# Three spill buffers, earlier first loads and rescheduled row operations in the last stage of a two-block transformer kernel

## Chip, cores and metric

The kernel runs on one core of a Trainium2 chip. The metric is the device time of one execution in microseconds (us); lower is better. The number compared is the median over several runs.

## What is computed

The reference applies two transformer blocks to a sequence of 512 tokens of width 1024, in float32. The first block has two kinds of attention and a mixture of experts; the second has a state space branch, an attention with forgetting and, last, a "PEER" layer. Only that last layer is touched by the change:

```python
def peer_ffn(h, w_query, sub_keys, u_tab, v_tab):     # 8 heads, 128 x 128 = 16384 experts, top 16
    q = (h @ w_query).reshape(bsz, seq, PEER_HEADS, 2, PEER_HALF)
    scores = jnp.einsum('blhcd,hckd->blhck', q, sub_keys)
    s_top, i_top = lax.top_k(scores, PEER_TOPK)
    # sums of all pairs of the two halves, then the best 16 pairs a head -> expert_idx, gates
    ...
        u_sel = u_tab[i_blk]
        act = jax.nn.gelu(jnp.einsum('td,thkd->thk', h_blk, u_sel))
        w = g_blk * act
        return jnp.einsum('thk,thkd->td', w, v_tab[i_blk])
```

## The kernel before

**Two ways through the same layer.** The 512 tokens are four tiles of 128. For three tiles (384 tokens, `DENSE`) the kernel computes all 16384 dot products with the table u, multiplies them by gates that are zero where an expert was not chosen, and multiplies the result w by the whole table v. The fourth tile (tile 0, `SPARSE`) is done by gathers: 128 selected rows of u and 128 of v for each token, one row per token at a time. Such a "row operation" (`row_work`) is one gather of 128 rows of 1024 float32, half a megabyte, issued by GpSimd (`gather`), and one multiply-accumulate on VectorE over 128x1024. There are 256 of them, 128 with u (L2486) and 128 with v (L2490).

**The loops.** Step n runs from 0 to 127. Steps 0 to 63 are the u loop, steps 64 to 127 the v loop (`NG` = 64). Each step needs one megabyte of a table: SyncE (its queue is called SP) loads it into one of two slots of `uv_raw` (`load`, two steps ahead), ScalarE copies it rounded into `uv_hi` (`high`, L2299), VectorE makes the remainder `uv_lo` (`low`, L2495), and TensorE multiplies in three passes (L123 to L125). A slot of `uv_raw` is free when `low` has read it; a slot of `uv_hi` when TensorE has finished the step two before.

**The u loop.** Each step gives two groups m of 128x384 activations. `gelu` (L2336, ScalarE) writes each into `a_out[:, m % NA, :]` and SP stores it to the DRAM tensor `a_rows`. Before `gelu(m)` may write, the store of m - NA must have landed, and TensorE must not start group m before `gelu(m - 2)`. In steps 0 to 45 VectorE selects experts (units "T" of `plan`), and in steps 22 to 58 VectorE, ScalarE and GpSimd make one-hot tables ("H", L2148 on GpSimd, L2471 and L2473 on VectorE) that TensorE multiplies into gates (L2245). ScalarE collects these in `spread` (L2310) and stores it twelve times, two megabytes each, to `g_rows`; the first write after such a store waits until it has landed.

**The v loop.** Step n = 64 + p needs w of pair p. SP loads the activations back (`a_rows` into a half of the old `qT4`, 384 KB for each p) and every fourth p also the gates of eight keys (`g_rows`, 1.5 MB), both by `load_weights(p)`. VectorE multiplies them (`wf`, L2505), ScalarE rounds (`w_hi`, L2303), VectorE subtracts (`w_lo`, L2510). `load_weights(p)` waits for `wf` of p - 2, whose slot it overwrites.

**The orders.** Each engine runs its instructions in program order, and so does each issuing queue. In its loop over n, SP issues `load(n + 2)`, then the two stores of step n, and then, from n = `NG - 2` on, `load_weights(n - (NG - 2))`. VectorE begins a step with `low(n + 1)`, then does the T and H work of that step, then the row operations that `plan` gives; in the v loop `weights` and one row operation stand between. GpSimd makes the one-hots of a step and then issues its gathers; a gather into a home waits for the VectorE operation that used this home before.

**The tables of numbers.** `rows_in` says how many row operations stand in each step. `MIDDLE_AT` and `LATE_AT` say from which row operation on the four homes in `keysT` and `work`, and the one in `rows_c`, may be used beside the five early ones: the first four are busy until the selection ends with step 45, the last until all gates are stored.

```python
    rows_in = {n: 1 for n in range(12, 22)} | {22: 3, 34: 4} | {n: 4 for n in range(46, NG)}
    rows_in |= {NG + k: 2 if k % 3 == 2 else 3 for k in range(NG - 1)}
```

Of the kernel before, what the change touches and what calls it, by code (L numbers as in the profile page):

```python
# [18 lines left out]
P = 128  # L19
# [16 lines left out]
PH, PK, PT16 = 8, 128, 16  # L36
# [39 lines left out]
def build_program(nc, t, out):  # L76
    with ExitStack() as ctx:
        emit(nc, t, out, ctx)


def emit(nc, t, out, ctx):
    era = []

    def sem(name):
        stack = ctx.enter_context(ExitStack())
        s = stack.enter_context(nc.semaphore(name))
        era.append((stack, s))
        return s

    def clear_semaphores():  # L90

        with nc.Block() as block:
            @block.gpsimd
            def _(pool):
                for _, s in era:
                    pool.sem_clear(s)
        for stack, _ in era:
            stack.close()
        era.clear()

    def sb(stack, name, shape, dt=F32):
        return stack.enter_context(nc.sbuf_tensor(name, shape, dt))
# [24 lines left out]
    class Gemm:  # L127
# [12 lines left out]
        def each(self, eng, body):  # L140

            base = 0
            for g, (count, width, _) in enumerate(self.segments):
                behind = self.segments[g + 1][1] if g + 1 < len(self.segments) else None
                if count > 1:
                    with eng.Fori(0, count - 1) as i:
                        body(i + base, g, i, width, width)
                body(base + count - 1, g, count - 1, width, behind)
                base += count
# [299 lines left out]
    stage = ExitStack()  # L449
# [387 lines left out]
    stage = ExitStack()  # L837
# [9 lines left out]
    stage = ExitStack()  # L847
# [332 lines left out]
    stage = ExitStack()  # L1180
    HW = KT // 2 * CH
    RAW, SPLIT, AHEAD, UNITS = 6, 3, 3, 12
# [286 lines left out]
    stage = ExitStack()  # L1469
# [63 lines left out]
    stage = ExitStack()  # L1533
# [22 lines left out]
    for at, kind in enumerate(CHUNKS):  # L1556
# [4 lines left out]
        for k in range(0, depth, per):  # L1561
            units.append((at, kind, src[:, k * width:(k + per) * width], range(k, k + per), width, k == 0, k + per == depth))
    NU = len(units)
    last_of = {at: x for x, (at, *_, last) in enumerate(units) if last}
    U_END, F_END, G0, Z0, Q0 = last_of[0], last_of[1], last_of[1] + 1, last_of[5] + 1, last_of[9] + 1
    s_ss, s_sq, s_root, s_g, s_h, s_tp, s_tpe, s_tph = (
# [377 lines left out]
    stage = ExitStack()  # L1944
# [42 lines left out]
    NG = P // GROUP  # L1987
# [9 lines left out]
    def uv_source(n):  # L1997
        return t["peer_u_2"][n, :, :] if n < NG else t["peer_v_2"][:, n - NG, :]
# [10 lines left out]
    stage = ExitStack()  # L2009
# [9 lines left out]

    stage = ExitStack()  # L2020
    uv_hi, uv_lo = (sb(stage, f"uv_{x}", [P, 2, GROUP * D], F32R) for x in ("hi", "lo"))
    NA = 2
    a_out = sb(stage, "a_out", [P, NA, DENSE])
    work = sb(stage, "work", [P, 8 * PT16 * PT16])
    rest = work[:, 0:8 * P].rearrange("p (n k) -> p n k", n=4)
# [1 line left out]
    match = work[:, :].rearrange("p (h k j) -> p h k j", h=PH, k=PT16)  # L2027
    top_s = sb(stage, "top_s", [P, 2 * PH, PT16])
    top_k = sb(stage, "top_k", [P, 2 * PH, PT16], U32)
    top_kf = sb(stage, "top_kf", [P, 2 * PH, PT16])  # L2030
    best_s = sb(stage, "best_s", [P, PH, PT16])
    best_p = sb(stage, "best_p", [P, PH, PT16], U32)
    part_p = sb(stage, "part_p", [P, PH, PT16], U32)
# [15 lines left out]
    with ExitStack() as routing:  # L2049
# [12 lines left out]
                                   "gates_spread", "gates_stored"))  # L2062
    s_ast = [sem(f"peer_act_stored{s}") for s in range(NA)]
    s_gin, s_ain = ([sem(f"peer_{x}{s}") for s in range(2)] for x in ("gates_here", "act_here"))
# [5 lines left out]
    EARLY = [x_sb[:, m, :] for m in range(1, TT)] + [rows_a[:, b, :] for b in range(2)]  # L2070
    MIDDLE = [keys_flat[:, b * D:(b + 1) * D] for b in range(2)] + [work[:, b * D:(b + 1) * D] for b in range(2)]
    LATE = [rows_c[:, 0, :]]
    MIDDLE_AT, LATE_AT = 20, 98
    homes = EARLY + MIDDLE + LATE
    s_row = [sem(f"row_here{b}") for b in range(len(homes))]
    home_of, use_of, before_of, last, uses = [], [], [], [-1] * len(homes), [0] * len(homes)
# [8 lines left out]
    turns_at = {x: [at + k for k in range(11)] for x, at in enumerate((0, 11, 23, 35))}  # L2085
    hots_in = [[2, 3, 3] * 4, [2, 3, 3] * 4, [2, 3] * 6 + [2]]
    hots_from = (22, 34, 46)
    rows_in = {n: 1 for n in range(12, 22)} | {22: 3, 34: 4} | {n: 4 for n in range(46, NG)}
    rows_in |= {NG + k: 2 if k % 3 == 2 else 3 for k in range(NG - 1)}
    plan, count, at = [[] for _ in range(2 * NG)], [0] * TT, 0  # L2090
    for x in range(TT):
        for n in turns_at[x]:
# [30 lines left out]
    for g in range(2 * SEL):  # L2123
        n = work_step[before_of[g]] if before_of[g] >= 0 else max(turns_at[SPARSE]) + 1
        if g >= MIDDLE_AT:
            n = max(n, max(turns_at[TT - 1]) + 1)
# [8 lines left out]
    with nc.Block() as block:  # L2135
# [38 lines left out]
        @block.sync  # L2174
        def _(sp):
            def load(n):
                if n >= 2:
                    sp.wait_ge(s_lo, n - 1)
                sp.dma_start(uv_raw[:, n % 2, :], uv_source(n)).then_inc(s_uv[n % 2], 16)

            def load_weights(p):
                if p == 0:
                    sp.wait_ge(s_scr, 4 * TT)
                    sp.wait_ge(s_gst, 16 * HALVES)
                if p >= 2:
                    sp.wait_ge(s_wf, p - 1)
                if p % (GKEYS // GROUP) == 0:
                    q = p // (GKEYS // GROUP)
                    sp.dma_start(g_in[:, q % 2, :].rearrange("p (h x) -> p h x", h=HALVES),
                                 g_rows.rearrange("h p x -> p h x")[:, :, q * GKEYS * HALF:(q + 1) * GKEYS * HALF])\  # L2190
                      .then_inc(s_gin[q % 2], 16)
                for m in (2 * p, 2 * p + 1):
                    sp.wait_ge(s_ast[m % NA], 16 * (m // NA + 1))
                sp.dma_start(a_in[:, p % 2, :, :], a_rows.rearrange("m p n -> p m n")[:, 2 * p:2 * p + 2, :])\
                  .then_inc(s_ain[p % 2], 16)

            for n in range(2 * NG):
                if n + 2 < 2 * NG:
                    load(n + 2)
                if n < NG:  # L2200
                    for m in (2 * n, 2 * n + 1):
                        sp.wait_ge(s_gelu, m + 1)
                        sp.dma_start(a_rows[m, :, :], a_out[:, m % NA, :]).then_inc(s_ast[m % NA], 16)
                if NG - 2 <= n < 2 * NG - 2:
                    load_weights(n - (NG - 2))
                if n == 2 * NG - 8:
                    sp.dma_start(x_back[:, :, :], x_rest).then_inc(s_xb, 16)
            outs = out.rearrange("a (m p) d -> p (a m) d", p=P)
            sp.wait_ge(s_rd, 2 * SEL)
            sp.dma_start(outs[:, 0, :], x_sb[:, 0, :]).then_inc(s_outd, 16)  # L2210
            for m in range(1, TT):
                sp.wait_ge(s_add, 2 * m)
                sp.dma_start(outs[:, m, :], x_back[:, m - 1, :]).then_inc(s_outd, 16)
            sp.wait_ge(s_outd, 16 * TT)
# [77 lines left out]
        def _(act):  # L2292
# [39 lines left out]
            def gelu(m):  # L2332
                act.wait_ge(s_pa, m + 1)
                if m >= NA:
                    act.wait_ge(s_ast[m % NA], 16 * (m // NA))
                act.activation(a_out[:, m % NA, :], ps[:, m % 2, 0:DENSE], ACT.Gelu_apprx_tanh).then_inc(s_gelu, 1)  # L2336
# [277 lines left out]
```

## Time and profile before

| | |
|---|---|
| median of 3 runs | 3783.2 us (3781.36 to 3788.04) |
| the profiled execution | 3781.3 us, of it the span of the trace 3779.5 us |
| u loop, first to last `uv_lo` | 2515 us to 3175 us from the span's start |
| v loop | 3183 us to the end |
| TensorE busy | 3353.4 us, 89% of the span |
| bytes moved by DMA | 954.87 MB, mean 253 GB/s |

The time is that of the whole kernel; the change touches its last third. A duration in the trace belongs to one profiled execution. TensorE's matmuls overlap, so a busy TensorE is not one at its peak; what counts is how far apart the steps are.

### The profile page before, as it was taken

To read this page: it belongs to the slowest core of one execution; us is meant where nothing else is said; L and a number is where in the kernel's file an instruction comes from. 1 tells how busy PE (TensorE), PEld (TensorE's weight loads), DVE (VectorE), ACT (ScalarE), POOL (GpSimd) and SP (SyncE) were. 2 spreads that over 40 slices of the span, in tenths; PEclk is the share of its full clock that TensorE was granted. 3 is DMA by queue.
4 is the path that set the end of the run, shared out by engine and by line. 5 is a ranking of instruction groups with operands and counts; after the bars stand their busy time and mean duration, and the time that the engine had idled before them with its cause. 6 is when DMAs were issued, how large, how long until landed. Compare 5 with 4: busy or idle time off the path is not lost. (4 is left out here: it accounts for less than half of the span.)

```text
span 3779.5 us, 46793 instructions
## 1 busy us (share of the span) xinstructions
PE 3353.4 (89%) x16253; PEld 2811.9 (74%) x16253; DVE 2726.5 (72%) x3557; ACT 1872.1 (50%) x2136; POOL 739.1 (20%) x524
## 2 busy tenths in 40 slices
PE   7697754999999999999299977799999996999998
PEld 3485543888888888887198856589999986777777
DVE  8316545999999999999444226348987776788887
ACT  1225413777777777777124334233478763333332
POOL 0000002011011011010200000001333585455552
PEclk9898867999999999999599978899999998999999
DMA  7520106999999999998633301235655699999996
GB/s 295 179 71 2 46 30 245 386 385 384 385 384 381 388 383 383 388 386 343 232 101 93 95 17 45 73 132 203 219 190 187 247 367 368 339 381 366 369 378 262
DMA packets 217466, 954.87 MB, mean 253 GB/s; under 512 B 23344, under 2 KB 85040, under 8 KB 142448
## 3 DMA queue, kind: packets, MB, share of 16 engines
q1 hardware_dynamic: 161872, 734.91, 51.9%
q0 software_dynamic: 46816, 167.80, 11.9%
q10 hardware_dynamic: 8640, 50.34, 3.3%
q8 instruction: 84, 1.38, 0.1%
q14 instruction: 54, 0.44, 0.0%
HBM read 864.92 MB, written 88.05 MB: 252 GB/s over the span
## 5 line engine op out<-in xcount | busy, mean ns | idle before, releaser
L1395 DVE TENSOR_TENSOR w_low<-w_raw,w_high 128x2048 fp32r<-128x2048 f32 x399 | 907.3, 2288 | 72.8 <-ACT w_high L1324 70.8
L1324 ACT ACTIVATE w_high<-w_raw 128x2048 fp32r<-128x2048 f32 x399 | 765.7, 1919 | 302.4 <-PE ps L125 162.4
L123 PE MATMUL ps<-w_high,xT_high 128*128 128x512 f32 x1056 | 428.8, 406 | 21.3 <-issue 21.3
L2495 DVE TENSOR_TENSOR uv_lo<-uv_raw,uv_hi 128x2048 fp32r<-128x2048 f32 x128 | 294.1, 2298 | 177.1 <-ACT uv_hi L2299 176.6
L124 PE MATMUL ps<-w_low,xT_high 128*128 128x512 f32 x1056 | 412.4, 391 | 0.0
L125 PE MATMUL ps<-w_high,xT_low 128*128 128x512 f32 x1056 | 412.3, 390 | 0.0
L123 PE MATMUL ps<-h4T_high,uv_hi 128*128 128x384 f32 x1024 | 353.5, 345 | 15.1 <-ACT a_out L2336 9.2
L123 PE MATMUL ps<-uv_hi,w_hi 128*128 128x512 f32 x768 | 305.2, 397 | 45.8 <-DVE w_lo L2510 24.9
L125 PE MATMUL ps<-h4T_high,uv_lo 128*128 128x384 f32 x1024 | 344.1, 336 | 0.0
L124 PE MATMUL ps<-h4T_low,uv_hi 128*128 128x384 f32 x1024 | 343.9, 336 | 0.0
L2299 ACT ACTIVATE uv_hi<-uv_raw 128x2048 fp32r<-128x2048 f32 x128 | 244.6, 1912 | 149.7 <-PE ps L125 120.5
L124 PE MATMUL ps<-uv_lo,w_hi 128*128 128x512 f32 x768 | 303.7, 395 | 0.0
L125 PE MATMUL ps<-uv_hi,w_lo 128*128 128x512 f32 x768 | 303.5, 395 | 0.0
L123 PEld LDWEIGHTS ps<-w_high,xT_high 128*128 128x128 f32 x1056 | 199.8, 189 | 60.1 <-issue 22.0
L1213 POOL COPY cur<-slot_ids 128x1 int32 (+1 forms) x34 | 41.1, 1210 | 1029.6 <-PE ps L1265 1026.2
L125 PEld LDWEIGHTS ps<-w_high,xT_low 128*128 128x128 f32 x1056 | 198.8, 188 | 42.6
L124 PEld LDWEIGHTS ps<-w_low,xT_high 128*128 128x128 f32 x1056 | 199.3, 189 | 39.6
L123 PE MATMUL ps<-w_high,hidT_high 128*128 128x512 f32 x528 | 218.1, 413 | 0.0
L123 PEld LDWEIGHTS ps<-h4T_high,uv_hi 128*128 128x128 f32 x1024 | 193.6, 189 | 18.8 <-DVE uv_lo L2495 7.9
L123 PEld LDWEIGHTS ps<-uv_hi,w_hi 128*128 128x128 f32 x768 | 147.1, 192 | 81.0 <-issue 50.5
L125 PE MATMUL ps<-w_high,hidT_low 128*128 128x512 f32 x528 | 206.3, 391 | 0.0
L124 PE MATMUL ps<-w_low,hidT_high 128*128 128x512 f32 x528 | 206.1, 390 | 0.0
(516 smaller groups left out, 7048.9 us busy)
## 6 DMA issues: line engine op xcount, KB each, us to landing
w_raw<-in_w_gate_up SPq DMA_DIRECT2D x267, 1024.0 KB, 6.8
w_raw<-in_w_down SPq DMA_DIRECT2D x132, 1024.0 KB, 7.2
uv_raw<-in_peer_u SPq DMA_DIRECT2D x64, 1024.0 KB, 5.4
uv_raw<-in_peer_v SPq DMA_DIRECT2D x64, 1024.0 KB, 9.5
wbuf_ada<-in_w_ada SPq DMA_DIRECT2D x12, 2048.0 KB, 8.7
a_rows<-a_out SPq DMA_DIRECT2D x128, 192.0 KB, 2.4
g_rows<-spread ACTq DMA_DIRECT2D x12, 2048.0 KB, 8.7
qT<-g_rows SPq DMA_DIRECT2D x16, 1536.0 KB, 15.1
```

The source lines that it names most:

```text
L123: pe.matmul(out, l_hi, r_hi, start=first, stop=False)
L124: pe.matmul(out, l_hi, r_lo, start=False, stop=False)
L125: return pe.matmul(out, l_lo, r_hi, start=False, stop=last)
L1213: pool.tensor_copy(cur[:, :], slot_ids[:, ds(j, 1)]).then_inc(s_cur, 1)
L1324: act.activation(w_hi[:, n % SPLIT, :], w_raw[:, n % RAW, :], ACT.Copy).then_inc(s_wh, 1)
L1395: dve.tensor_tensor(w_lo[:, n % SPLIT, :], w_raw[:, n % RAW, :], w_hi[:, n % SPLIT, :].bitcast(F32), ALU.subtract).then_inc(s_wl, 1)
L2299: act.activation(uv_hi[:, n % 2, :], uv_raw[:, n % 2, :], ACT.Copy).then_inc(s_hi, 1)
L2495: dve.tensor_tensor(uv_lo[:, n % 2, :], uv_raw[:, n % 2, :], uv_hi[:, n % 2, :].bitcast(F32), ALU.subtract).then_inc(s_lo, 1)
```

## The change

Seven numbers or places change. `a_out` has three slots instead of two, and the copy `top_kf` of the selected keys is written over `top_s` instead of having memory of its own. `rows_in` has one row operation in each of the steps 12 to 45 (four in steps 22 and 34), then three and four in turn up to step 63, then two and three in turn. Counted out, steps 12 to 45 hold 40 row operations instead of 17, steps 46 to 63 hold 63 instead of 72, and the v loop holds 153 instead of 167. `MIDDLE_AT` and `LATE_AT` follow. `load_weights(p)` stands one step earlier in SP's program, and ahead of that step's stores instead of behind them.

```diff
-    NA = 2
+    NA = 3
...
-    top_kf = sb(stage, "top_kf", [P, 2 * PH, PT16])
+    top_kf = top_s
...
-    MIDDLE_AT, LATE_AT = 20, 98
+    MIDDLE_AT, LATE_AT = 44, 112
...
-    rows_in = {n: 1 for n in range(12, 22)} | {22: 3, 34: 4} | {n: 4 for n in range(46, NG)}
-    rows_in |= {NG + k: 2 if k % 3 == 2 else 3 for k in range(NG - 1)}
+    rows_in = {n: 1 for n in range(12, 46)} | {22: 4, 34: 4} | {n: 3 + n % 2 for n in range(46, NG)}
+    rows_in |= {NG + k: 3 if k % 2 else 2 for k in range(NG - 1)}
...
+            AHEAD = 3
             for n in range(2 * NG):
                 if n + 2 < 2 * NG:
                     load(n + 2)
+                if NG - AHEAD <= n < 2 * NG - AHEAD:
+                    load_weights(n - (NG - AHEAD))
                 if n < NG:
                     for m in (2 * n, 2 * n + 1):
                         sp.wait_ge(s_gelu, m + 1)
                         sp.dma_start(a_rows[m, :, :], a_out[:, m % NA, :]).then_inc(s_ast[m % NA], 16)
-                if NG - 2 <= n < 2 * NG - 2:
-                    load_weights(n - (NG - 2))
```

SP's queue where the u loop ends, before the change, from the loading of u's last slice (the first row) on. `in_peer_v` is the table v; the gates and activations of p = 0 are the rows that write `qT`:

```order
L2179 DMA uv_raw<-in_peer_u 128x2048
L2203 DMA a_rows<-a_out 128x384 x2
L2179 DMA uv_raw<-in_peer_v 128x2048
L2203 DMA a_rows<-a_out 128x384 x2
L2189 DMA qT<-g_rows 128x12x256
L2194 DMA qT<-a_rows 128x2x384
L2179 DMA uv_raw<-in_peer_v 128x2048
L2203 DMA a_rows<-a_out 128x384 x2
L2194 DMA qT<-a_rows 128x2x384
L2179 DMA uv_raw<-in_peer_v 128x2048
```

The same place after the change:

```order
L2179 DMA uv_raw<-in_peer_u 128x2048
L2189 DMA qT<-g_rows 128x12x256
L2194 DMA qT<-a_rows 128x2x384
L2206 DMA a_rows<-a_out 128x384 x2
L2179 DMA uv_raw<-in_peer_v 128x2048
L2194 DMA qT<-a_rows 128x2x384
L2206 DMA a_rows<-a_out 128x384 x2
L2179 DMA uv_raw<-in_peer_v 128x2048
L2194 DMA qT<-a_rows 128x2x384
L2206 DMA a_rows<-a_out 128x384 x2
```

The gates and the activations of p = 0 have moved ahead of two pairs of stores and of the first slice of v; throughout the v loop `load_weights(p)` now stands ahead of `load(p + 64)` instead of behind it.

VectorE in the middle of the u loop, from the last one-hots of step 27 over the whole of step 28, before the change:

```order
L2471 TENSOR_SCALAR first_hot<-iota_row,selT 128x128
L2473 TENSOR_TENSOR second_hot<-iota_row,selT 128x512
L2495 TENSOR_TENSOR uv_lo<-uv_raw,uv_hi 128x2048
L2397 MAX best_s<-work 128x8 x4
L2400 MAX_INDEX best_p<-best_s,work 128x8 x4
L2417 TENSOR_TENSOR work<-top_s 128x256 x4
L2386 MAX best_s<-work 128x8 x4
L2471 TENSOR_SCALAR first_hot<-iota_row,selT 128x128
L2473 TENSOR_TENSOR second_hot<-iota_row,selT 128x512
```

The same stretch after the change:

```order
L2472 TENSOR_SCALAR first_hot<-iota_row,selT 128x128
L2474 TENSOR_TENSOR second_hot<-iota_row,selT 128x512
L2487 SCALAR_TENSOR_TENSOR rows_a,row_dot<-rows_a,h_s 128x1024
L2496 TENSOR_TENSOR uv_lo<-uv_raw,uv_hi 128x2048
L2398 MAX best_s<-work 128x8 x4
L2401 MAX_INDEX best_p<-best_s,work 128x8 x4
L2418 TENSOR_TENSOR work<-top_s 128x256 x4
L2387 MAX best_s<-work 128x8 x4
L2472 TENSOR_SCALAR first_hot<-iota_row,selT 128x128
L2474 TENSOR_TENSOR second_hot<-iota_row,selT 128x512
```

One row operation (L2487) now stands between the last one-hots of a step and the next `uv_lo`; the work of the selection is the same.

GpSimd's queue after step 22, before the change; the 64 one-hots are those of steps 23 to 45:

```order
L2163 DMA x_sb<-in_peer_u_rows,row_id 128x1024 x3
L2148 TENSOR_SCALAR first_hot<-iota_row,selT 128x128 x32
L2163 DMA rows_a<-in_peer_u_rows,row_id 128x1024 x2
L2148 TENSOR_SCALAR first_hot<-iota_row,selT 128x128 x32
L2163 DMA keysT<-in_peer_u_rows,row_id 128x1024 x2
L2163 DMA work<-in_peer_u_rows,row_id 128x1024 x2
```

The same place after the change, the first few of those steps:

```order
L2163 DMA rows_a<-in_peer_u_rows,row_id 128x1024 x2
L2148 TENSOR_SCALAR first_hot<-iota_row,selT 128x128 x2
L2163 DMA x_sb<-in_peer_u_rows,row_id 128x1024 x3
L2163 DMA rows_a<-in_peer_u_rows,row_id 128x1024
L2148 TENSOR_SCALAR first_hot<-iota_row,selT 128x128 x3
L2163 DMA rows_a<-in_peer_u_rows,row_id 128x1024
L2148 TENSOR_SCALAR first_hot<-iota_row,selT 128x128 x3
L2163 DMA x_sb<-in_peer_u_rows,row_id 128x1024
L2148 TENSOR_SCALAR first_hot<-iota_row,selT 128x128 x2
```

Between the one-hots of two steps GpSimd now issues a gather, which waits for the row operation that used its home before.

## Rows read from the trace of the kernel before

**Rows 1.** Windows: bounds and length, busy us, clock, DMA share, GB/s.

```profile
2717.00:2984.00 267.00, 258.08 (x1669) 254.40 (x1668) 223.15 (x591) 212.50 (x387) 96.55 (x68) 1.00 0.52 190
2984.00:3188.00 204.00, 185.51 (x1138) 182.09 (x1136) 150.93 (x223) 128.23 (x222) 162.76 (x107) 0.98 0.93 356
3188.00:3210.00 22.00, 1.17 (x4) 0.83 (x3) 4.12 (x6) 2.78 (x3) 5.51 (x5) 0.57 1.04 399
...
3240.00:3745.00 505.00, 480.00 (x2066) 393.41 (x2065) 419.21 (x364) 158.70 (x117) 246.81 (x149) 0.98 0.99 371
```

**Rows 2.** Timeline of ScalarE in the v loop: start, us; idle before, releaser.

```profile
3261.26 1.92 ACT L2299 ACTIVATE uv_hi<-uv_raw 128x2048 fp32r<-128x2048 f32 x1 [2.17 <-PE ps L125]
...
3269.42 1.92 ACT L2299 ACTIVATE uv_hi<-uv_raw 128x2048 fp32r<-128x2048 f32 x1 [2.17 <-PE ps L125]
...
3281.07 1.91 ACT L2299 ACTIVATE uv_hi<-uv_raw 128x2048 fp32r<-128x2048 f32 x1 [1.50 <-DMA uv_raw<-in_peer_v]
```

**Rows 3.** All `uv_lo` from 3230.5 to 3750 us: first and last start.

```profile
L2495 DVE TENSOR_TENSOR uv_lo<-uv_raw,uv_hi x60: 2281/2293/2296, 3230.6 to 3749.0; 128x2048 fp32r<-128x2048 f32 x60
```

**Rows 4.** Waits in the v loop, 3240 to 3745 us: total, times, longest.

```profile
DVE wf L2505 <- DMA qT<-a_rows: 26.3, 10, 4.7
PE ps L123 <- DVE w_lo L2510: 24.9, 10, 4.6
```

**Rows 5.** Timeline of SP in the v loop around one load of gates.

```profile
3257.37 0.34 SPq L2179 DMA_DIRECT2D uv_raw<-in_peer_v  x1
3258.23 0.36 SPq L2189 DMA_DIRECT2D qT<-g_rows  x1
3258.69 8.87 SPq L2194 DMA_DIRECT2D qT<-a_rows  x1
3267.60 0.59 SPq L2179 DMA_DIRECT2D uv_raw<-in_peer_v  x1
```

**Rows 6.** DMA from 3240 to 3740 us: total, queues, issue to landing.

```profile
DMA packets 67717, 186.29 MB, mean 373 GB/s; under 512 B 4515, under 2 KB 40867, under 8 KB 60195
...
q1 hardware_dynamic: 45946, 106.78, 58.7%
q0 software_dynamic: 21747, 79.18, 40.8%
...
qT<-g_rows SPq DMA_DIRECT2D x14, 1536.0 KB, 15.1
```

**Rows 7.** Timeline of VectorE where the v loop begins.

```profile
3183.34 2.29 DVE L2495 TENSOR_TENSOR uv_lo<-uv_raw,uv_hi 128x2048 fp32r<-128x2048 f32 x1
...
3188.98 1.22 DVE L2486 SCALAR_TENSOR_TENSOR x_sb<-x_sb,h_s 128x1024 f32<-128x1024 f32 x1
...
3206.14 0.96 DVE L2505 TENSOR_TENSOR wf<-qT 128x768 f32<-128x768 f32 x1 [15.93 <-DMA qT<-a_rows]
3208.00 0.96 DVE L2510 TENSOR_TENSOR w_lo<-wf,w_hi 128x768 fp32r<-128x768 f32 x1 [0.91 <-ACT w_hi L2303]
```

**Rows 8.** Waits where the v loop begins, 3186 to 3240 us.

```profile
PE ps L123 <- issue: 20.8, 1, 20.8
```

**Rows 9.** Timeline of SP, 3176 to 3212 us.

```profile
3180.89 0.38 SPq L2189 DMA_DIRECT2D qT<-g_rows  x1
```

**Rows 10.** Waits late in the u loop, 2985 to 3188 us.

```profile
ACT spread L2310 <- DMA g_rows<-spread: 28.6, 4, 10.2
...
ACT a_out L2336 <- DMA a_rows<-a_out: 8.5, 2, 7.3
```

**Rows 11.** Waits in steps 23 to 45, 2724 to 2984 us.

```profile
POOL first_hot L2148 <- PE ps L2245: 155.9, 53, 5.1
DVE uv_lo L2495 <- ACT uv_hi L2299: 37.1, 17, 4.5
...
PE ps L2245 <- DVE second_hot L2473: 6.1, 7, 1.4
```

**Rows 12.** A row operation on VectorE, ns least, median and most.

```profile
L2486 DVE SCALAR_TENSOR_TENSOR x_sb<-x_sb,h_s x47: 1208/1218/1300, 2631.1 to 3338.0; 128x1024 f32<-128x1024 f32 x47
```

## Prediction

> **What bounds the kernel now.** I read the last third stretch by stretch, first in the windows. From 2984 us on the DMA engines are busy all the time (shares 0.93, 1.04, 0.99), while in the middle of the u loop they are half idle (0.52) [rows 1]. So from step 47 on the question is which bytes arrive in time; before that it is whether TensorE is fed.
>
> The v loop has a floor. Two `uv_hi` that each waited for TensorE start at 3261.26 and 3269.42, 8.16 us apart; the second after that waits for the loading of v and comes 11.65 us later instead of 8.16 [rows 2]. Over the loop, 60 `uv_lo` go from 3230.6 to 3749.0 us: 59 steps of 8.79 us [rows 3]. At 8.16 us they would take 481.4 us, so 37.0 us are lost there. TensorE waits for `w_lo`, and `wf` for the activations, ten times each, 24.9 and 26.3 us [rows 4]; a load of gates stands at the head of such a wait. The one of p = 8 is issued at 3258.23, behind a slice of v of 3257.37, and the issue of the activations behind it takes 8.87 us because the queue is full [rows 5]. Gates need 15.1 us to land [rows 6], and two steps are 16.3.
>
> Where v begins, TensorE stands still for 20.8 us once [rows 8]. VectorE is done with its four row operations at 3188.98 + 1.2 = 3190.2, and `wf` starts at 3206.14, after waiting 15.93 us for the activations [rows 7]; the gates ahead of them had been issued only at 3180.89 [rows 9], because SP first had to wait for the GELUs of step 62.
>
> Late in the u loop TensorE is busy 185.5 of 204 us [rows 1], so 18.5 us are idle. The longest waits on ScalarE are for the store of `spread`, 28.6 us in four, and for the store of `a_out`, 8.5 us in two [rows 10]. In steps 23 to 45 hardly anything waits: TensorE 6.1 us for one-hots; VectorE idles 37.1 us for `uv_hi` [rows 11].
>
> **The change part by part.**
>
> *Fewer row operations late.* 14 leave the v loop. One is 0.524 MB. The software queue moved 79.18 MB in 40.8% of 500 us, thus at 388 GB/s; the other moved 106.78 MB in 58.7%, at 364 GB/s [rows 6]. A row operation therefore takes 1.35 us of all sixteen engines, 14 take 18.9 us. As DMA is the bound there, this is the most that the bytes give; VectorE's time (14 at 1.2 us [rows 12]) lies beside it. The floor by TensorE, 37.0 us away, does not cut it. But the order of the queue changes too (below), so I take 14 us, between 0 and 18.9.
>
> On bandwidth the Trainium skill, DMA: Bandwidth & Descriptors, section Specifications, gives about 358 GB/s as the limit of HBM for one core. The trace has a mean of 373 GB/s in this stretch [rows 6], so it differs and the measurement decides; by 358 GB/s an operation would take 1.46 us as an estimate, and 14 of them 20.5 us, too little more to matter.
>
> *Nine fewer in steps 46 to 63.* They free 9 x 1.35 = 12.2 us of DMA where TensorE is idle 18.5 us. Not all of this idle time is the DMA's: the wait for `spread` stays, with one buffer, though its store lands sooner. The third slot of `a_out` takes away at most the 8.5 us on ScalarE, and half of that would come back, because the next `uv_raw` is late as well in a full queue. I take 8 us for both, between 0 and 14.
>
> *Where v begins.* The gates of p = 0 are issued before the stores of step 61, when the last `spread` is stored; that is some 16 to 20 us earlier than 3180.89, two steps less what the full queue costs. What is late next is VectorE: `uv_lo` of step 64 starts at 3183.34, the four operations end at 3190.2, and from the start of `wf` to the end of `w_lo` it takes 3208.00 + 0.96 - 3206.14 = 2.8 us [rows 7]: w is ready at 3193 at best, while TensorE ended near 3188. About 5 us of the 20.8 stay, so 15.8 can go. The clock adds to it: in the stall TensorE is granted 0.57 [rows 1], between its levels of 1.2 and 2.4 GHz, and a short stall lets less of that follow. Against it, the early gates (1.57 MB) and activations go ahead of the slice of v for step 64, and at 364 GB/s their 2 MB take 5.4 us of a queue shared with the gathers. I take 12 us, between 4 and 18.
>
> *The queue order in the v loop.* `load_weights(p)` waits for `wf` of p - 2 as before and so is issued at the same moment, but the slice of v for step p + 64 now stands behind it. Activations land 1.05 MB earlier, the slice later. The sum of bytes to land before the step is the same. `wf` could be 16.3 us after the gates' issue, the slice must be there about a microsecond sooner. This is why I count 14 of the 18.9 us above.
>
> *23 more row operations in steps 12 to 45.* On VectorE 23 x 1.22 = 28.1 us [rows 12]. Below: its idle time before `uv_lo` in steps 23 to 45 is 37.1 us [rows 11], and `uv_lo` is needed a step of TensorE later, which hides all of it: 0. Above: the idle time does not always lie where the operations go (17 waits in 22 steps), and TensorE's waits for one-hots, seven of them [rows 11], could each grow by one operation: 7 x 1.22 = 8.5 us. Behind the waiting row operation stands the next `uv_lo`, then the one-hots. The gathers lie in half idle DMA. On GpSimd a gather now waits for the operation of its step, and the one-hots of the next stand behind it; GpSimd idles 155.9 us there, ahead of TensorE [rows 11], and 23 gathers of under 2 us fit. I take a loss of 4 us, nearer to the waits that exist than to none.
>
> *At nothing:* `top_kf` over `top_s` is the same copy on an engine that runs in order, and no value of `top_s` is read afterwards. SP's wait for the gates' store at step 61 holds back stores of `a_out`; the third slot covers that. If the cover were too short, `gelu` would stall as it does now.
>
> **Sum.** 14 + 8 + 12 - 4 = 30 us. The profiled execution took 3781.3 us (span 3779.5 and 1.8 around it), so 3751.3; the median of the runs is 1.9 us above that execution, so 3753 us. A check from the bytes: 23 row operations, 31 us of DMA work, leave the saturated stretch, and it has idle time to win back: 0.07 of 204 us is 14 [rows 1]. Together 45, somewhat over the 34 that the three gains sum to.
>
> **The rivals.**
>
> *A, as above:* 3743 to 3765, chance 0.58.
>
> *B, the bytes only move.* The stall where v begins is removed, but in it DMA moved 399 GB/s [rows 1] and filled every slot; without it the v loop starts with nothing ahead and pays it back. Then only the bytes count: 31 us at most, and less if those of the late u loop lay beside the waits for `spread`. 18.9 less 4 in the middle less a few for the tighter slice is about 12 us, 3771 (3765 to 3778). For it: DMA is never idle at 0.99. Against: the stall has a cause in SP's order that is gone. Chance 0.16.
>
> *C, everything reaches its floor.* v nearer 8.16 us a step as soon as DMA no longer binds (18.9), 17 where it begins, 14 late in u, no loss: 50 us, 3733 (3728 to 3745). Chance 0.12.
>
> *D, the slice of v is late behind the gates: slower.* Before, the four steps of one load of gates take 4 x 8.79 = 35.2 us, 2.5 more than 4 x 8.16 [rows 2, 3]. Now the slice is issued behind an issue that can take 8.87 us [rows 5], about 9 us later than before, with 2 MB ahead of it, and must be there a microsecond sooner than `wf`. If each of the fifteen groups loses 2 us more than I counted, the 30 us are gone; if 3.7 more, that is 55 us, and the kernel takes 3753 + 55 = 3808. It decides from about 2 us a group. For it: the order puts a small urgent load ahead of a large one that is just as urgent. Against: the gates land before two steps are over, and the slice is then alone. Chance 0.07.
>
> A rule of the Trainium skill speaks for D: DMA: Bandwidth & Descriptors, section Queues, rings and completion order, says that each engine consumes a ring's descriptors in order and takes turns between queues by packets. By it the reordering wins no bandwidth, and a slice behind the gates cannot pass them. That agrees with the late slice in rows 5 and 2, issued at 3267.60 and awaited until 3281.07.
>
> *E, nothing:* the middle pays 28.1 us in full because VectorE has no slack where it matters, and it eats the gains: 3783 - 34 + 28 = 3777, within the bound below. Chance 0.07.
>
> **How the numbers follow.** Within 0.2%, 7.6 us, a measurement can't be told from no change. Faster takes A, B and C, 0.86; same takes E, 0.07; slower is D, 0.07. The range leaves out D, the far half of C and what of E and B lies above 3778: 3734 to 3778; A's own is 3743 to 3765.
>
> **What would show it.** The windows and waits of the changed kernel: the stall of 20.8 us falls to 5 to 9. `wf` no longer waits for activations at the gates' steps, or much less; `uv_hi` waits for v instead. The steps of v come to 8.5 to 8.6 us. The waits of ScalarE for the store of `a_out` are gone. Steps 23 to 45 take 0 to 8 us more, with `uv_lo` no longer waiting. I would be wrong if v's steps stay at 8.8, with waits of `uv_hi` for the slice three times the present, or if TensorE's waits for one-hots in the middle exceed 20 us.

## The result

The change made the kernel slower: 3831.95 us (median of 4 runs, 3818.79 to 3837.36) against 3783.76 us of the kernel before in the same session (4 runs, 3781.36 to 3788.04), a ratio of 1.0128 with a 95% interval of 1.0106 to 1.0150. The profiled execution of the changed kernel is the fastest of its runs, 3818.8 us with a span of 3817.0, so the two traces explain 37.5 of the 48 us between the medians.

The windows of the changed kernel, with the columns of [rows 1]:

```profile
2717.00:2990.00 273.00, 261.72 (x1664) 258.69 (x1663) 249.27 (x635) 212.89 (x387) 130.85 (x92) 0.98 0.65 232
2990.00:3190.00 200.00, 186.12 (x1137) 183.55 (x1135) 135.57 (x200) 127.03 (x221) 145.27 (x96) 0.97 0.93 352
3190.00:3213.00 23.00, 13.29 (x50) 10.82 (x51) 15.79 (x19) 6.24 (x6) 10.66 (x7) 0.78 0.93 348
3240.00:3782.00 542.00, 491.40 (x2038) 399.66 (x2037) 397.63 (x332) 155.19 (x114) 208.95 (x135) 0.94 0.89 325
```

Against [rows 1] the v loop (last row) has a DMA share of 0.89 instead of 0.99 and 325 instead of 371 GB/s, and a granted clock of 0.94 instead of 0.98. The engines move less, and something else holds the steps. All `uv_lo` of the v loop from step 67 on, count, first and last start:

```profile
L2496 DVE TENSOR_TENSOR uv_lo<-uv_raw,uv_hi x60: 2283/2292/2294, 3220.4 to 3786.5; 128x2048 fp32r<-128x2048 f32 x60
```

59 steps take 566.1 us, 9.59 each, instead of 8.79 [rows 3]. From the starts of `uv_lo` the two traces part like this (us, before and after): steps 23 to 46, 266.7 and 273.2; 46 to 61, 176.0 and 169.9; 61 to 64, 30.6 and 37.5; 64 to 67, 47.2 and 30.4; 67 to 122, 478.7 and 530.7; 122 to 127, 47.9 and 43.6. These 55 steps of the v loop lose 52 us, and everything else together wins 14.

The waits of the v loop (total, times, longest):

```profile
DVE uv_lo L2496 <- ACT uv_hi L2300: 141.7, 42, 6.9
...
ACT uv_hi L2300 <- DMA uv_raw<-in_peer_v: 106.7, 28, 7.3
...
PE ps L123 <- DVE w_lo L2511: 50.6, 15, 4.4
```

`wf`, which had waited for activations ten times [rows 4], waits no more. In its place `uv_hi` waits for the slices of v, 28 times and 106.7 us. SP around one load of gates, where [rows 5] had the slice ahead of it:

```profile
3407.12 0.36 SPq L2189 DMA_DIRECT2D qT<-g_rows  x1
3407.58 0.73 SPq L2194 DMA_DIRECT2D qT<-a_rows  x1
3408.36 0.81 SPq L2179 DMA_DIRECT2D uv_raw<-in_peer_v  x1
...
3415.69 0.47 SPq L2179 DMA_DIRECT2D uv_raw<-in_peer_v  x1
...
3428.51 0.47 SPq L2179 DMA_DIRECT2D uv_raw<-in_peer_v  x1
```

The gates, then the activations, then 0.7 us later the slice for step 88. ScalarE over the same stretch (start, us; idle before and what ended it):

```profile
3410.15 1.92 ACT L2300 ACTIVATE uv_hi<-uv_raw 128x2048 fp32r<-128x2048 f32 x1 [2.17 <-PE ps L125]
...
3422.96 1.92 ACT L2300 ACTIVATE uv_hi<-uv_raw 128x2048 fp32r<-128x2048 f32 x1 [6.82 <-DMA uv_raw<-in_peer_v]
...
3430.25 1.92 ACT L2300 ACTIVATE uv_hi<-uv_raw 128x2048 fp32r<-128x2048 f32 x1 [1.30 <-DMA uv_raw<-in_peer_v]
```

The slice issued at 3408.36 is there at 3422.96, 14.6 us later; ScalarE idled 6.82 us for it. Between the issue of the gates and that moment, 15.8 us, SP's queue moved 3.36 MB and the gathers' queue 1.82 MB. The next slice, issued at 3415.69, also takes 14.6 us. TensorE then stood 4.14 us and came back at half clock; windows of 6 us (busy TensorE with its matmuls first, granted clock third from the end):

```profile
3418.00:3424.00 6.00, 6.00 (x28) 4.95 (x28) 0.52 (x1) 1.04 (x1) 1.07 (x2) 1.00 1.02 407
3424.00:3430.00 6.00, 2.37 (x11) 1.64 (x9) 5.05 (x5) 1.72 (x2) 0.23 (x1) 0.95 0.70 265
3430.00:3436.00 6.00, 5.49 (x13) 4.36 (x14) 5.89 (x6) 1.92 (x1) 5.01 (x3) 0.50 0.97 367
3436.00:3442.00 6.00, 6.00 (x27) 4.90 (x27) 3.29 (x4) 1.13 (x2) 2.35 (x2) 0.98 0.95 336
```

28 matmuls in 6 us at clock 1.00, 13 at 0.50, 27 at 0.98. The clock was at its lower level of 1.2 GHz right after the stall. In the 5.49 us that TensorE was busy there, full clock gives 25.6 matmuls; the 12.6 that are missing, of 6/28 us each, cost 2.7 us on top of the 4.

Where v begins, waits and SP's timeline (compare [rows 8, 9]):

```profile
PE ps L123 <- issue: 10.9, 2, 10.7
ACT a_out L2337 <- DMA a_rows<-a_out: 10.3, 2, 7.4
```

```profile
3161.22 0.38 SPq L2189 DMA_DIRECT2D qT<-g_rows  x1
3161.70 10.25 SPq L2194 DMA_DIRECT2D qT<-a_rows  x1
3172.00 1.17 SPq L2206 DMA_DIRECT2D a_rows<-a_out  x2
3173.21 0.88 SPq L2179 DMA_DIRECT2D uv_raw<-in_peer_v  x1
```

The gates of p = 0 are issued at 3161.22 instead of 3180.89, and the long stall is 10.7 instead of 20.8 us. But the issue of the activations behind them blocks SP for 10.25 us, the slice of v for step 64 is issued only at 3173.21, and `a_out` still waits for its store, 10.3 us in two, with three slots. Of the signs that the prediction named, one came as forecast (`wf` no longer waits), the stall stayed above its 5 to 9 us, and two came that were to show it wrong: steps above 8.8 us, and waits of `uv_hi` for the slices more than three times as long (17.4 us in thirteen from 3200 to 3757 us before, 106.7 now).

### The profile page after: what moved, and what is told of

Its sections match the earlier page's. It is cut to its first block and busy times, and to the rows that moved or that the text cites. A ratio compares the mean times of both kernels' runs of the same rounds, so it can differ in the third digit from the quotient of the medians.

```text
span 3817.0 us, 46793 instructions
## 1 busy us (share of the span) xinstructions
PE 3376.3 (88%) x16253; PEld 2829.4 (74%) x16253; DVE 2724.4 (71%) x3557; ACT 1871.3 (49%) x2136; POOL 722.9 (19%) x524
## 5 line engine op out<-in xcount | busy, mean ns | idle before, releaser
L123 PE MATMUL ps<-h4T_high,uv_hi 128*128 128x384 f32 x1024 | 355.7, 347 | 17.4 <-ACT a_out L2337 10.4
```

The costliest lines, as they stand in the source:

```text
L123: pe.matmul(out, l_hi, r_hi, start=first, stop=False)
```

## The experiments

Theory Q: the order of SP's queue makes v slow. Its rivals: the new table of row operations does (R), or the shift of memory addresses. The step times below are (last start - first start) / (count - 1) of the `uv_lo` in the window from 3240 to 3740 us; by this count the kernel before has 8.76 us (58 from 3238.7 to 3738.2) and the changed one 9.68 (52 from 3239.9 to 3733.6). This window does not hold the same steps in every kernel, and in the fast ones it takes in the end of v, where few gathers are left. The next table has the same 55 steps of each trace, `uv_lo` 67 to 122, in us:

| before | changed | 1 | 2 | 3 | 4 | 5 | 6 | 7 | 8 | 9 | 10 | 11 | 12 |
|---|---|---|---|---|---|---|---|---|---|---|---|---|---|
| 478.7 | 530.7 | 481.4 | 529.0 | 481.6 | 481.6 | 483.5 | 453.8 | 476.2 | 451.5 | 496.4 | 465.8 | 455.8 | 513.1 |

**1. Old order, all else new.**

```diff
-                if NG - AHEAD <= n < 2 * NG - AHEAD:       # ahead of the stores
-                    load_weights(n - (NG - AHEAD))
+                if NG - 2 <= n < 2 * NG - 2:               # behind them
+                    load_weights(n - (NG - 2))
```

> The changed kernel with the loads of weights back at their old place (two steps ahead, behind the slice of v and behind the stores); three buffers and the new table of row operations stay. Theory Q (the queue order costs: each slice of v stands behind the activations and gates and behind their wait for wf): the v loop returns to 8.5 to 8.7 us a step from 9.60, the stall of 20 us where v begins comes back, the whole takes about 3765 us (3755 to 3778). Theory R (the new table of row operations, two and three in turn, makes the v loop slow): it stays near 3832, with steps of 9.6.

Measured: 3775.0 us against 3780.8, ratio 0.9978 (0.9965 to 0.9991).

```profile
L2495 DVE TENSOR_TENSOR uv_lo<-uv_raw,uv_hi x57: 2283/2292/2295, 3246.8 to 3734.0; 128x2048 fp32r<-128x2048 f32 x57
```

56 steps of 8.70 us. Theory Q holds, R falls. The rest of the change is worth about 6 us; the time lies within what was expected, 10 us above its centre. The stall where v begins comes back, but with 15.9 instead of 20.8 us.

**2. New order alone, on the kernel before.** The same edit the other way round.

> The kernel before with only the loads of weights moved three steps ahead and ahead of the step's stores. Theory Q: steps of v of 9.6 to 9.9 us, the stall where v begins shorter by 8 to 12 us, the whole 3820 to 3850. Theory R: no slower than before, 3770 to 3784.

Measured: 3835.7 us, ratio 1.0144 (1.0127 to 1.0161).

```profile
L2495 DVE TENSOR_TENSOR uv_lo<-uv_raw,uv_hi x52: 2281/2292/2295, 3245.2 to 3732.0; 128x2048 fp32r<-128x2048 f32 x52
```

9.55 us a step, and from step 64 to 67 31.0 us instead of 47.2, while steps 61 to 64 take 43.9 instead of 30.6. Both directions agree: the order alone costs the whole loss.

**3. The table of row operations alone.**

```diff
-    MIDDLE_AT, LATE_AT = 20, 98
+    MIDDLE_AT, LATE_AT = 44, 112
-    (rows_in of before)
+    (rows_in of the change)
```

> The kernel before with only the new table of row operations (with the two numbers for the homes). Theory Q: 14 fewer row operations in v save up to 18.9 us, fewer late in u some more, the middle loses up to 6: 3758 to 3775. Theory R: slower, 3800 or more.

Measured: 3772.0 us against 3780.8, ratio 0.9967 (0.9953 to 0.9981). Steps 23 to 46 take 273.4 us, 6.7 more than before. The v loop:

```profile
3240.00:3740.00 500.00, 478.13 (x2063) 392.08 (x2063) 403.85 (x337) 159.62 (x116) 212.03 (x136) 0.98 0.97 358
```

```profile
L2495 DVE TENSOR_TENSOR uv_lo<-uv_raw,uv_hi x58: 2282/2292/2295, 3242.4 to 3739.8; 128x2048 fp32r<-128x2048 f32 x58
```

8.73 us a step instead of 8.76, with 358 instead of 373 GB/s [rows 6]. Steps 67 to 122 have nine row operations less, 4.7 MB, and take 481.6 us instead of 478.7: something other than bytes held them. The v loop as a whole, steps 64 to 127, does win 9.0 us (564.8 instead of 573.8), but in its first three steps (42.4 instead of 47.2) and its last five (40.8 instead of 47.9). Steps 46 to 61 take 169.4 us instead of 176.0.

**4. The third buffer alone.**

```diff
-    NA = 2
+    NA = 3
-    top_kf = sb(stage, "top_kf", [P, 2 * PH, PT16])
+    top_kf = top_s
```

> The kernel before with only the third slot of a_out and the copy of the keys written over top_s. Both theories: within 0.2% of before, 3776 to 3784, the waits of ScalarE for the store of a_out gone. If the shift of the memory addresses mattered, it would show here.

Measured: 3784.2 us against 3780.8, ratio 1.0005 (0.9993 to 1.0017). The waits of `gelu` for the store are gone from the list of the late u loop, and nothing is won. The waits of `uv_hi` for its slices of u are 13.9 us there, where they were 11.3.

**5. The wait alone.** The new order does two things to a slice of v: SP reaches it only after its wait for `wf`, and its bytes stand behind others.

```diff
                 if n + 2 < 2 * NG:
+                    if n >= NG:
+                        sp.wait_ge(s_wf, n - NG + 1)
                     load(n + 2)
```

> The kernel before with one wait added: in the v loop SP issues a slice of v only when wf of the step has been made, as the new order forces it to, but no transfer stands ahead of the slice that did not before. Theory W (the wait on wf, 1.3 us later at each slice, is the price of the new order): steps of v near 9.6 and 3825 or more. Theory B (the bytes of activations and gates ahead of the slice are the price): steps of 8.8 to 9.0, 3783 to 3798. I hold B for likelier.

Measured: 3786.6 us against 3786.3, ratio 1.0009 (0.9996 to 1.0022); 57 `uv_lo` from 3238.9 to 3732.9, 8.82 us a step. The wait costs nothing that these runs can tell, at most 8 us by the interval.

**6. The changed kernel with small gates.**

```diff
+                    hs = HALVES if q < 2 else 1
-                    sp.dma_start(g_in[...all 12 parts...], g_rows[...all 12 parts...])
+                    sp.dma_start(g_in[...parts 0:hs...], g_rows[...parts 0:hs...])
```

> The changed kernel, but from the third load of gates on only one twelfth of each is loaded (the rest of the gates is left as it stood, so the output is not the reference's; no other work is left out). Theory B with the gates as its main part: the v loop falls from 9.60 to 8.3 to 8.6 us a step, 3765 to 3775. Theory W: it stays at 9.3 or more, 3810 or more.

Measured: 3749.1 us against 3786.3, ratio 0.9902 (0.9876 to 0.9927).

```profile
L2497 DVE TENSOR_TENSOR uv_lo<-uv_raw,uv_hi x60: 2280/2294/2295, 3242.8 to 3729.9; 128x2048 fp32r<-128x2048 f32 x60
```

8.26 us a step, near the floor of 8.16, and a time 16 us below what I expected, with wait, activations and order as in the changed kernel. The loss of the changed kernel hangs on the gates. But the edit also takes 20 MB out of the loop, so by itself it can't say whether their place costs or their bytes; experiment 8 does, which keeps the bytes.

**7. Only the first two loads early.**

```diff
-                if NG - AHEAD <= n < 2 * NG - AHEAD:
+                if n in (NG - 3, NG - 2):
                     load_weights(n - (NG - 3))
...                                                         # behind the stores
+                if NG <= n < 2 * NG - 2:
+                    load_weights(n - (NG - 2))
```

> Three buffers and the new table of row operations, with the loads of weights of p = 0 and 1 at their new early place and all the others at the old one. Theory: the time of the version with the old order, 3775, less the 8 to 12 us that the early place wins where v begins: 3763 to 3768. Rival: what is won there is paid back in the first steps of v, 3772 to 3777.

Measured: 3771.9 us against 3786.3, ratio 0.9961 (0.9948 to 0.9973); 8.64 us a step. Against experiment 1 the intervals overlap. In the traces steps 64 to 67 fall from 42.5 to 30.7 us and steps 61 to 64 rise from 28.8 to 40.5: together 71.3 and 71.2. The early loads move time from steps 64 to 67 into the three steps ahead of them and win nothing that these runs can show.

**8. Gates three steps earlier, behind a slice.** Experiment 7, and the load of gates taken out of its place at p = 4q and put behind the activations of p = 4q - 3; its slot is free then, since `wf` of p = 4q - 5 has been waited for.

```diff
+            def load_gates(q):
+                (the same DMA of g_rows into g_in)
             def load_weights(p):
...
-                if p % (GKEYS // GROUP) == 0:
-                    (load of gates q = p // 4)
+                if p == 0:
+                    load_gates(0)
                 (load of the activations of p)
+                if p % 4 == 1 and p + 3 < NG:
+                    load_gates((p + 3) // 4)
```

> As the version with the first two early, and each load of gates is issued three steps earlier, behind the activations of p = 4q - 3, as soon as its slot is free. Theory L (the v loop loses its 35 us because the gates are issued two steps before use and need 15): steps of 8.2 to 8.4, 3735 to 3748. Theory D (the DMA engines are full, whatever the order): steps stay at 8.7, 3763 to 3768.

Measured: 3750.6 us against 3786.3, ratio 0.9907 (0.9884 to 0.9929).

```profile
3240.00:3740.00 500.00, 495.85 (x2178) 409.04 (x2177) 419.72 (x352) 165.98 (x121) 218.10 (x138) 1.00 0.96 364
```

```profile
L2501 DVE TENSOR_TENSOR uv_lo<-uv_raw,uv_hi x60: 2283/2294/2295, 3242.8 to 3731.1; 128x2048 fp32r<-128x2048 f32 x60
```

8.28 us a step and the clock at 1.00 all through. Theory L holds by the steps, though the whole is 3 us above its range; D, by which the order can't matter, falls. The mean of 364 GB/s takes in the end of v: the last 54 us of this window have 188 GB/s, and steps 67 to 122 have 383. SP around one load of gates:

```profile
3465.80 0.35 SPq L2179 DMA_DIRECT2D uv_raw<-in_peer_v  x1
3466.67 0.36 SPq L2196 DMA_DIRECT2D qT<-a_rows  x1
3467.07 0.47 SPq L2182 DMA_DIRECT2D qT<-g_rows  x1
3473.95 1.71 SPq L2179 DMA_DIRECT2D uv_raw<-in_peer_v  x1
```

The slice that follows the gates is issued 6.9 us after them.

**9. The changed kernel with the gates behind the slice.**

```diff
                     load(n + 2)
+                if (a load of gates was due at n - 1):
+                    load_gates(...)
                 if NG - AHEAD <= n < 2 * NG - AHEAD:
                     load_weights(n - (NG - AHEAD))          # without gates, but for p = 0
```

> The changed kernel, but from the second load of gates on each stands behind the slice of v that it had been put ahead of; the activations stay ahead, and so does the wait on wf. Theory G (of all that the new order puts ahead of the slice, only the 1.5 MB of gates cost): the v loop falls from 9.60 to 8.6 to 8.8 us a step, 3765 to 3776. Theory A (the activations and the wait together cost a part): 9.0 or more, 3790 or more.

Measured: 3789.8 us against 3782.1, ratio 1.0014 (0.9996 to 1.0032); 9.08 us a step (56 from 3238.7 to 3738.1). Its waits in the v loop:

```profile
ACT uv_hi L2304 <- DMA uv_raw<-in_peer_v: 35.3, 14, 5.0
DVE wf L2510 <- DMA qT<-g_rows: 33.4, 12, 4.0
```

Most of the loss is gone, and not all. The gates are issued as early as in the kernel before and again behind the slice, but the activations now stand ahead of it; `wf` waits for the gates (33.4 us in twelve), and slices are late as well. Steps 67 to 122 take 15 us more than in experiment 1, which has the same table. Beside small gates (6) the activations and the wait cost nothing of this kind. That is theory A by the steps; the time is just below its 3790 and 14 us above the range of G.

**10. Gates earlier on the kernel before,** with its own table and two buffers: the edit of experiment 8 alone, behind the old order.

> The kernel before, with its own table of row operations and two buffers, and each load of gates but the first issued three steps earlier. Theory L (v loses its time to the gates' lateness, not to bandwidth): steps of 8.2 to 8.3 although 14 more row operations are in the loop, the whole 3750 to 3760. Theory D (the bytes matter once the gates are in time): 8.4 to 8.6 a step, 3765 to 3775.

Measured: 3764.5 us against 3782.1, ratio 0.9959 (0.9945 to 0.9974).

```profile
L2499 DVE TENSOR_TENSOR uv_lo<-uv_raw,uv_hi x59: 2282/2292/2295, 3244.6 to 3739.1; 128x2048 fp32r<-128x2048 f32 x59
```

8.53 us a step at 372 GB/s (steps 67 to 122: 382). The steps are theory D's, the whole just below its range. Once the gates are in time the bytes do matter: 8.53 with 167 row operations in v, 8.28 to 8.31 with 153.

**11. Experiment 8 without the early loads of p = 0 and 1.**

> Three buffers, the new table of row operations, the loads of weights at the old place, and each load of gates but the first three steps earlier: the version that took 3750.6 without its early loads of p = 0 and 1. If those win nothing (the stall is only moved), it takes the same, 3747 to 3754; if they win something, 3755 to 3762.

Measured: 3751.4 us against 3782.1, ratio 0.9915 (0.9882 to 0.9949), 8.31 us a step (60 from 3240.0 to 3730.2). The same as experiment 8: the early loads win nothing.

**12. The changed kernel, gates three steps earlier, still right ahead of a slice.** The edit of experiment 8 on the changed kernel's order.

> The changed kernel, and each load of gates but the first is issued three steps earlier, with the activations of p = 4q - 3, so that again a slice of v is issued right behind it. Theory F (what costs is the slice of v issued right behind the 1.5 MB, whenever that is): the v loop stays at 9.3 to 9.7 us a step, 3810 or more. Theory L (earliness alone counts): 8.3 to 8.5 a step, 3750 to 3760, as the version in which the same load stands behind a slice, just as early.

Measured: 3803.2 us against 3781.0, ratio 1.0052 (1.0034 to 1.0071); the profiled execution took 3813.0.

```profile
L2500 DVE TENSOR_TENSOR uv_lo<-uv_raw,uv_hi x54: 2282/2292/2314, 3240.2 to 3738.8; 128x2048 fp32r<-128x2048 f32 x54
```

```profile
3422.41 0.67 SPq L2182 DMA_DIRECT2D qT<-g_rows  x1
3423.13 1.65 SPq L2179 DMA_DIRECT2D uv_raw<-in_peer_v  x1
```

9.41 us a step. The gates are as early as in experiment 8, but a slice is issued 0.7 us after them instead of 6.9. By the step time this is theory F, by the median it lies 7 us below F and 43 above L. The profiled execution is the slowest of its runs, where that of the changed kernel was the fastest of its own; the medians, 3803.2 and 3832.0 us, say that the lead alone wins back some 29 us. A slice with a step between it and the gates wins 42 without the lead (9), and both together 81 (8). So neither theory holds alone: the place costs most, and the lead counts as well.

## Why the prediction was wrong

The forecast was 30 us faster; it came 48 us slower, outside the range, on the side of rival D, which had 0.07.

Two steps of the working failed. One turned the sign; by the other a gain was counted that could not show.

**The price of the order turned the sign**: "I take 14 us" instead of 18.9, so about 5 stood for it, on this ground: "The sum of bytes to land before the step is the same." It cost 52 us in 55 steps, 3.8 us a group of four, and experiments 1 and 2 show that the order alone carries it. Experiments 5, 6, 8, 9 and 12 narrow the mechanism down: not the wait (5), not the activations by themselves (6), not the bytes as such (8), but 1.5 MB of gates right ahead of a slice that has two steps (34 of the 52 us go when they stand behind it in 9). Two things stay open: why an earlier issue wins a part even with the slice right behind (12), and why the activations ahead of the slice cost 15 us beside full gates (9) and nothing beside small ones; 12 and 8 differ in the place of the activations as well, so a part of what parts them may be this. Against D it had been argued that the slice "is then alone". It is not: gates and activations, 2 MB, are ahead of it in SP's queue and the gathers beside it, and it takes 14.6 us from issue to use.

Rival D had this mechanism, though not its reason for it: the slice is issued 2.1 us after its slot is free (`uv_lo` of step 86 ends at 3406.23, the issue is at 3408.36), not 9 us later. That 3.8 us a group met the 3.7 that it tried as an example is luck. Its total of 3808 is 24 us short of the measured one, 13 in the two traces, because it still counted 14 us for the bytes; the rest is that the profiled execution was a fast one.

**The bound of the v loop was misread**: "As DMA is the bound there, this is the most that the bytes give." The windows of steps 67 to 122 (columns as in [rows 1]) for the kernel before, the changed one and experiments 3, 10 and 8:

```profile
3230.60:3709.30 478.70, 458.64 (x1981) 376.50 (x1980) 398.25 (x348) 152.33 (x112) 244.31 (x148) 0.98 1.00 372
3220.40:3751.10 530.70, 479.12 (x1981) 389.74 (x1981) 386.04 (x327) 152.09 (x111) 214.94 (x139) 0.94 0.90 329
3225.60:3707.10 481.50, 459.63 (x1981) 376.51 (x1980) 387.26 (x326) 152.17 (x111) 216.68 (x139) 0.98 0.98 362
3228.30:3694.10 465.80, 454.19 (x1988) 373.28 (x1988) 397.24 (x349) 152.01 (x112) 238.55 (x148) 1.00 1.01 382
3234.60:3686.10 451.50, 450.76 (x1986) 372.37 (x1986) 386.85 (x326) 152.27 (x111) 220.31 (x139) 1.00 1.01 383
```

With the gates early, three kernels (8, 10, 11) move 381 to 383 GB/s. At 382 the 178.1 MB of the kernel before need 466 us, and it took 478.7: it was held 12 us above what its bytes need by the gates, issued two steps before their use with 15.1 us to land [rows 6]. Experiment 3 lowered the need of the bytes to 456 us (174.1 MB) and its steps did not move. Experiment 10 took the lateness away and came down to 465.8, the bytes' time; experiment 8 took both and ended at 451.5, with TensorE busy for 450.8 of it. So the size of the term was right: with the gates in time the fewer row operations are worth 13 us (3764.5 and 3751.4 us in 10 and 11, where the third buffer also differs). What the sum lacked is the condition.

**Where the 52 us lie on TensorE.** In the rows above it does the same 1981 matmuls before and after. It idles 51.6 instead of 20.1 us and is busy 479.1 instead of 458.6: 31.5 us are the stalls and 20.5 the lower clock behind them (mean 0.94 instead of 0.98). The clock stands in no term of the v loop.

**Where v begins**: 12 us expected, and steps 61 to 67 went from 77.9 to 67.9 us, 10. That the size is near is luck, for the reason is not right. The old order with the new table has 71.3 there (experiment 1), and the early loads add nothing to it (7 and 11). The stall falls from 20.8 to 10.7 us, but the three steps ahead of it grow, because the slice for step 64 stands behind the gates. That was rival B, for this place.

**Late u**: 8 us expected. 6.1 us in steps 46 to 61 in the changed kernel, 6.6 in experiment 3, but 0.6 in experiment 1 and a loss of 3 to 4 in experiments 7 and 8. The profiles with the new table have 169.4 to 180.1 us there, those with the old one 175.7 to 182.6, so it stays open whether anything was won. The third buffer by itself wins nothing (4).

**The middle**: 4 us expected, 6.5 in the changed kernel (266.7 to 273.2) and 4 to 7 in all profiles with the new table, within its bounds. From 2717 to 2990 us `uv_lo` waits 17.8 us, where it had 37.1 [rows 11], TensorE's waits for these one-hots are 8.0 instead of 6.1, and GpSimd, which had idled for TensorE, now waits for row operations:

```profile
POOL x_sb L2163 <- DVE x_sb L2487: 76.1, 12, 8.7
...
DVE uv_lo L2496 <- ACT uv_hi L2300: 17.8, 11, 4.4
...
PE ps L2246 <- DVE second_hot L2474: 8.0, 7, 2.1
```

**The sum's check from the bytes** repeated the error and could not find it: it assumed that the engines were the bound.

Two statements of the Trainium skill, DMA: Bandwidth & Descriptors, stood in the prediction. The one of section Queues, rings and completion order, that each engine consumes a ring's descriptors in order, fits experiments 8 and 12, which differ by where a slice stands behind the gates (451.5 and 513.1 us). The limit of about 358 GB/s in section Specifications was already passed in the kernel before, 373 [rows 6], and experiment 8 has 383 over 451.5 us.

**The best version** found is experiment 8, or the simpler 11: 0.9907 and 0.9915 of the kernel before, 31 to 36 us faster, where the change as made is 48 us slower.

## What to carry to other kernels

A DMA share near 1 doesn't say that bytes are the bound. Take some bytes out, or look for one late transfer at every stall, before pricing a change by bandwidth; a term for bytes may be right in size and still come to nothing until the late transfer is gone. In a queue with slots of two, look at what is issued right ahead of the transfer with the least slack. In this kernel a large load belonged where a whole step lay between it and the next tight one; a larger lead won 29 us with that neighbour in place and 81 without it. Price a periodic stall of TensorE at more than its length where the trace shows half clock behind it.

## What the hardware showed

Over the same 55 steps the DMA share was 0.98, 1.00 and 1.01 at 362, 372 and 383 GB/s (experiment 3, the kernel before, experiment 8), so it hardly tells how much more would fit. A load of 1.05 MB issued right behind 1.5 MB of gates and 0.4 MB of activations took 14.6 us to its use. The issue of the activations on SP took 0.73 us behind the gates at 3407.58 in the changed kernel, and 8.87 us behind a slice and the gates issued within 1.3 us [rows 5]. A stall of TensorE of 4 us was followed by a window of 6 us at a granted clock of 0.50, 2.7 us lost again; over the 55 steps the changed kernel lost 31.5 us more to stalls and 20.5 to the clock behind them. Without such stalls the clock was 1.00 over 500 us (experiment 8).
